# Gate chunks of the modulation move from the weight ring to a ring of three slots on Pool's queue

## What is computed

```python
mod = jax.nn.silu(c) @ w_ada[layer] + b_ada[layer]
shift, scale, gate = jnp.split(mod, 3, axis=-1)
h = rms_norm(x, norm_gain[layer]) * (1.0 + scale[:, None, :]) + shift[:, None, :]
proj = h @ w_in[layer]
q_sb, k_sb, v_sb, z_sb, q_r, k_r, v_r, z_r = jnp.split(proj, split_at, axis=-1)
...            # stick-breaking attention of q_sb, k_sb, v_sb; retention of q_r, k_r, v_r
y = jnp.concatenate([oa, ob], axis=-1).astype(x.dtype) @ w_out[layer]
x = x + (gate[:, None, :] * y).astype(x.dtype)
```

## Time and profile before

| what | value |
|---|---|
| median of three runs | 1970.38 us (1968.21 to 1970.95) |
| profiled execution | 1965.76 us, span 1963.9 us |
| PE busy | 1808.8 us (92%) |
| DVE busy | 1260.0 us (64%) |
| ACT busy | 904.1 us (46%) |
| mean granted clock of PE | 0.961 |
| DMA issue of a weight chunk of `w_in`, 512 KB | lands after 3.8 us (median) |
| DMA issue on POOL's queue into `ada_ring`, 512 KB | lands after 5.9 us (median) |
| DMA issue of `con1`, 836 KB | lands after 5.7 us |

### The profile page before, as it was taken

How to read it: one execution, slowest core, us unless ns; L and a number is a source line. 1 busy time by engine, 2 the same in 40 slices (tenths; PEclk the granted TensorE clock), 3 DMA queues, 4 the chain that set the end, 5 groups by cost and what they waited for, 6 DMA issues and landing times.

```text
span 1963.9 us, 23699 instructions
## 1 busy us (share of the span) xinstructions
PE 1808.8 (92%) x9667; PEld 1531.2 (78%) x9667; DVE 1260.0 (64%) x1604; ACT 904.1 (46%) x1158; POOL 101.3 (5%) x114
## 2 busy tenths in 40 slices
PE   5799987788778998999999999999989999999897
PEld 4688876576556787888888888888878888888786
DVE  5789954564545765578757666785465557667654
ACT  4344432343334543466544456664444555454542
POOL 2311100000000000000000000000000000000000
PEclk8899998899988999999999999999989999999898
DMA  7899955554444454666655455656546565444453
GB/s 263 327 313 342 310 160 186 175 161 150 150 134 123 140 189 144 173 191 191 183 165 148 140 162 160 179 165 193 185 142 187 162 190 151 137 119 119 129 188 112
DMA packets 311835, 350.52 MB, mean 178 GB/s; under 512 B 11232, under 2 KB 286816, under 8 KB 311728
## 3 DMA queue, kind: packets, MB, share of 16 engines
q1 hardware_dynamic: 302400, 315.12, 52.8%
q0 software_dynamic: 9328, 33.89, 4.7%
HBM read 346.87 MB, written 2.10 MB: 178 GB/s over the span
## 4 chain that ended last, share of the span: by engine, by line
PE 77%; DMA 8%; DVE 6%; ACT 5%; issue 3%; SPq 0%; POOL 0%; DVEq 0%; ACTq 0%
PE psG L475 42%; PE psG L476 21%; DMA raw<-in_w_in 7%; ACT w_hi L405 3%; PE psG L469 2%; PE psG L471 2%; PE psG L470 2%; DVE w_lo L409 2%; DVE gate_sum L1145 1%; PE psH L1720 1%; DMA raw<-in_mem_w 1%; PE psH L1734 1%; PE psH L1709 1%; PE psH L2014 1%; PE psH L2015 1%
## 5 line engine op out<-in xcount | busy, mean ns | idle before, releaser
L475 PE MATMUL psG<-xA,w_hi 128*128 128x512 f32 x3392 | 1237.4, 407 | 44.7 <-issue 19.7
L409 DVE TENSOR_TENSOR w_lo<-raw,w_hi 128x1024 fp32r<-128x1024 f32 (+1 forms) x560 | 686.7, 1236 | 438.1 <-ACT w_hi L405 436.3
L476 PE MATMUL psG<-xA,w_lo 128*128 128x256 f32 x3392 | 960.7, 283 | 0.0
L475 PEld LDWEIGHTS psG<-xA,w_hi 128*128 128x128 f32 x3392 | 649.6, 192 | 210.2 <-issue 37.1
L405 ACT ACTIVATE w_hi<-raw 128x1024 fp32r<-128x1024 f32 (+1 forms) x560 | 574.7, 1045 | 493.3 <-DMA raw<-in_w_in 282.5
L476 PEld LDWEIGHTS psG<-xA,w_lo 128*128 128x128 f32 x3392 | 653.4, 193 | 4.2 <-issue 3.6
L444 ACT ACTIVATE P<-psG 128x512 f32<-128x512 f32 x102 | 60.6, 594 | 200.9 <-PE psG L476 200.9
L1098 DVE TENSOR_TENSOR P<-psG,P 128x512 f32<-128x512 f32 (+2 forms) x103 | 70.3, 683 | 106.8 <-ACT P L444 104.6
L1145 DVE SCALAR_TENSOR_TENSOR ada_sum<-ada_ring,silc,ada_sum 128x1024 f32<-128x1024 f32 x60 | 79.5, 1330 | 0.0
L566 POOL TENSOR_TENSOR W<-W 128x512 f32<-128x512 f32 x15 | 22.2, 1483 | 1018.9 <-ACT W L619 1018.9
L475 PE MATMUL psG<-xB,w_hi 128*128 128x512 f32 x192 | 67.6, 396 | 0.0
(11 more groups left out here) (304 smaller groups left out, 1772.1 us busy)
## 6 DMA issues: line engine op xcount, KB each, us to landing
raw<-in_w_in SPq DMA_DIRECT2D x360, 512.0 KB, 3.8
raw<-in_w_out SPq DMA_DIRECT2D x128, 512.0 KB, 3.4
ada_ring<-in_w_ada POOLq DMA_DIRECT2D x64, 512.0 KB, 5.9
raw<-in_mem_w SPq DMA_DIRECT2D x32, 512.0 KB, 8.1
raw<-in_w_ada SPq DMA_DIRECT2D x32, 512.0 KB, 3.9
raw<-in_w_uq SPq DMA_DIRECT2D x24, 384.0 KB, 3.3
raw<-in_w_ukv SPq DMA_DIRECT2D x32, 128.0 KB, 2.4
raw<-in_w_ukv SPq DMA_DIRECT2D x16, 256.0 KB, 3.3
```

The source lines that it names most:

```text
L409: nc.vector.tensor_tensor(low(n), low(n, raw), high(n), ALU.subtract).then_inc(lo_ready, 1)
L475: nc.tensor.matmul(psG[:, bank + f, :], hi[:, w], x, start=first, stop=False)
L476: last = nc.tensor.matmul(psG[:, bank + f, S:2 * S], lo[:, w], x[:, 0:S], start=False, stop=end)
```

## The change

The weight ring holds weights alone. `raw` gets seven slots and `w_hi` five (twelve in all, as before). ACT, before it writes `w_hi` for chunk n, waits until chunk n - 5 is used. The 32 gate chunks are appended to the list that POOL loads; they use three of its six slots, tiles 48, 52 and 56 (`GATE_RING` = 3), and POOL waits for the last user of a slot. DVE's adds stand at other places: every second chunk of `G_SBQK` (8), every chunk of `G_SBV` (8), every second of `G_RTQK` (8), the first eight of `G_RTV` (8). The columns of the first half follow `G_SBV` directly, without the wait for `sb_y` 2; those of the second half follow `G_RTV`, behind the wait for `sb_y` 4 that stood there. As the retention values are written where gate chunks lie, ACT waits for all 96 adds before it takes a product of `G_RTV` (`before_taken`). At the start, `first()` comes before the inverse root on ACT and before the norm on DVE.

```diff
-SLOTS = 6
+SLOTS, HIGH_SLOTS = 7, 5
+GATE_RING = 3
-        w_hi = sb("w_hi", [NP, SLOTS, 1024], F32R)
+        w_hi = sb("w_hi", [NP, HIGH_SLOTS, 1024], F32R)
-        GATE_AT = {G_SBQK: lambda i: i % 2 == 1, G_SBV: lambda i: i % 2 == 1, G_RTQK: lambda i: i % 4 == 3,
-                   G_RTV: lambda i: i % 2 == 1, G_SBZ: lambda i: i % 2 == 1}
+        GATE_AT = {G_SBQK: lambda i: i % 2 == 1, G_SBV: lambda i: True, G_RTQK: lambda i: i % 2 == 1, G_RTV: lambda i: i < 8}
+        ITEMS = [("weight", n) for n in range(len(CHUNKS))]
+        ADA_SLOT = [m % len(ADA_RING) for m in range(2 * ADA_HALF)] + [m % GATE_RING for m in range(ADA_HALF)]
...
                 if j >= SLOTS:
-                    before, m = ITEMS[j - SLOTS]
-                    sp.wait_ge(*((chunk_used, m + 1) if before == "weight" else (ada_used, 2 * ADA_HALF + m + 1)))
-                if kind == "gate":
-                    k, half = m_to_gate(n)
-                    sp.dma_start(raw[:, j % SLOTS, :], ada_rows(k, 2, half)).then_inc(raw_loaded[j % SLOTS], 16)
-                    continue
+                    sp.wait_ge(chunk_used, ITEMS[j - SLOTS][1] + 1)
...
         def split_hi(act, n):
             arrived(act, "weight", n)
+            if n >= HIGH_SLOTS:
+                act.wait_ge(chunk_used, n + 1 - HIGH_SLOTS)
...
-                if m >= len(ADA_RING):
-                    pool.wait_ge(ada_used, m + 1 - len(ADA_RING))
+                if ADA_BEFORE[m] is not None:
+                    pool.wait_ge(ada_used, ADA_BEFORE[m] + 1)
                 pool.dma_start(ada_ring[slot][:, :], ada_rows(k, part, half)).then_inc(ada_loaded[slot], 16)
...
+            first()
             norm_inverse_root(0)
-            first()
...
-            run(G_RTV, lambda b, p: sb_hook(2 + b, p))
+            run(G_RTV, lambda b, p: sb_hook(2 + b, p), before_taken=lambda: act.wait_ge(ada_used, 3 * ADA_HALF))
...
-            norm(0, mem_raw, V("mem_norm", 0, 16), between=between)
+            first()
+            norm(0, mem_raw, V("mem_norm", 0, 16))
...
             run_products(pe, G_SBV)
+            gate_columns(0)
             pe.wait_ge(loaded["con1"], 16)
...
             run_products(pe, G_RTQK, sb_hook)
-            pe.wait_ge(q["sb_y"], 2)
-            gate_columns(0)
             run_products(pe, G_RTV, lambda b, p: sb_hook(2 + b, p))
             pe.wait_ge(q["sb_y"], 4)
+            gate_columns(1)
...
             run_products(pe, G_SBZ, rt_hook)
-            pe.wait_ge(q["rt_y"], 2)
-            gate_columns(1)
```

More of the change, by code:

```diff
@@ L338, in build @@
         BLOCKS = [(g, b) for g in ORDER for b in range(g.blocks)]
-        GATE_AT = {G_SBQK: lambda i: i % 2 == 1, G_SBV: lambda i: i % 2 == 1, G_RTQK: lambda i: i % 4 == 3,
-                   G_RTV: lambda i: i % 2 == 1, G_SBZ: lambda i: i % 2 == 1}
[L343 to L348, removed]
+        GATE_AT = {G_SBQK: lambda i: i % 2 == 1, G_SBV: lambda i: True, G_RTQK: lambda i: i % 2 == 1, G_RTV: lambda i: i < 8}
+        GATE_UNITS = [g.c0 + i for g in ORDER if g in GATE_AT for i in range(len(g.order)) if GATE_AT[g](i)]
+        ITEMS = [("weight", n) for n in range(len(CHUNKS))]
         PLACE, LOADS = {}, []
         for j, (kind, n) in enumerate(ITEMS):
-            by_tile = kind == "weight" and CHUNKS[n][0].by_tile
+            by_tile = CHUNKS[n][0].by_tile
             LOADS.append((LOADS[j - SLOTS] if j >= SLOTS else 0) + (CHUNKS[n][0].kk if by_tile else 1))
             PLACE[kind, n] = j
+        ADA_SLOT = [m % len(ADA_RING) for m in range(2 * ADA_HALF)] + [m % GATE_RING for m in range(ADA_HALF)]
+        ADA_BEFORE = [max([i for i in range(m) if ADA_SLOT[i] == ADA_SLOT[m]], default=None) for m in range(3 * ADA_HALF)]
+        ADA_COUNT = [ADA_SLOT[:m + 1].count(ADA_SLOT[m]) for m in range(3 * ADA_HALF)]
         def arrived(eng, kind, n):
@@ L369, in high @@
             g = CHUNKS[n][0]
-            return w_hi[:, n % SLOTS, 0:g.kk * g.cols]
+            return w_hi[:, n % HIGH_SLOTS, 0:g.kk * g.cols]
         def low(n, t=None):
@@ L398, in ada_rows @@
             return io["w_ada"][NP * k:NP * k + NP, c0:c0 + D_MODEL // 2]
-        def m_to_gate(m):
-            return m % KT, m // KT
         def split_hi(act, n):
             arrived(act, "weight", n)
+            if n >= HIGH_SLOTS:
+                act.wait_ge(chunk_used, n + 1 - HIGH_SLOTS)
             nc.scalar.activation(high(n), low(n, raw), ACT.Copy).then_inc(hi_ready, 1)
@@ L489, in build @@
         sb_v, rt_v = (tiles(t, 8).rearrange("p (h f) -> p h f", h=2) for t in (SBV, RTV))
-        ADA_ORDER = [(half, k, part) for half in range(2) for k in range(KT) for part in range(2)]
+        ADA_ORDER = [(half, k, part) for half in range(2) for k in range(KT) for part in range(2)] + [
+            (half, k, 2) for half in range(2) for k in range(KT)]
         GATED1 = [(SBQ, SBZ), (SBQ + 4, SBZ + 4), (RTQ, RTZ), (RTQ + 4, RTZ + 4)]
@@ L571, in _ @@
             for m, (half, k, part) in enumerate(ADA_ORDER):
-                slot = m % len(ADA_RING)
+                slot = ADA_SLOT[m]
                 if m == 20:
                     add_squares(1)
-                if m >= len(ADA_RING):
-                    pool.wait_ge(ada_used, m + 1 - len(ADA_RING))
+                if ADA_BEFORE[m] is not None:
+                    pool.wait_ge(ada_used, ADA_BEFORE[m] + 1)
                 pool.dma_start(ada_ring[slot][:, :], ada_rows(k, part, half)).then_inc(ada_loaded[slot], 16)
@@ L670, in first, with run, block_done @@
                     split_hi(act, n)
-            def run(g, hook=no_hook, hook_first=True):
-                run_split(act, split_hi, g, hook, hook_first, lambda b: take_product(act, g, b))
+            def run(g, hook=no_hook, hook_first=True, before_taken=lambda: None):
+                def block_done(b):
+                    before_taken()
+                    take_product(act, g, b)
+                run_split(act, split_hi, g, hook, hook_first, block_done)
             act.wait_ge(loaded["vec"], 16)
@@ L1070, in norm_step, with norm @@
                                                in1=x[:, 0:S], op0=ALU.add, op1=ALU.subtract).then_inc(q["nm_lo"], 1)
-            def norm(n, src, gain, between=None):
+            def norm(n, src, gain):
                 dve.wait_ge(q["nm_rs"], n + 1)
                 for t in range(KT + 2):
-                    if between:
-                        between(t)
                     norm_step(n, src, gain, None, t, 0, KT)
@@ L1125, in ada_add @@
             def ada_add(m):
[L1127 to L1140, removed]
+                half, k, part = ADA_ORDER[m]
+                dve.wait_ge(ada_loaded[ADA_SLOT[m]], 16 * ADA_COUNT[m])
+                src, out = ada_ring[ADA_SLOT[m]][:, :], ada_sum[:, part, :] if part < 2 else gate_sum[:, :]
+                if k == 0 and half:
+                    dve.wait_ge(q["ada_cols" if part < 2 else "gate_cols"], 1)
                 if k == 0:
@@ L1146, in ada_add @@
                                            op1=ALU.add).then_inc(ada_used, 1)
-            def between(t):
-                if t == 4:
-                    first()
-            norm(0, mem_raw, V("mem_norm", 0, 16), between=between)
+            first()
+            norm(0, mem_raw, V("mem_norm", 0, 16))
             def modulation(half):
@@ L1199, in hook @@
                     if p % 2 and GATE_AT[g](i):
-                        ada_add(2 * ADA_HALF + ITEMS[PLACE["weight", g.c0 + i] + 1][1])
+                        ada_add(2 * ADA_HALF + GATE_UNITS.index(g.c0 + i))
                 return hook
@@ L1304, in z1_hook @@
                     gate_1(n - 1)
-            run(G_SBZ, both(z1_hook, gate_hook(G_SBZ)))
-            gate_columns(1)
+            run(G_SBZ, z1_hook)
             run(G_RTZ, lambda b, p: z1_hook(2 + b, p))
```

## The result

| | before | after |
|---|---|---|
| median | 1969.3 us | 1844.2 us |
| profiled execution, span | 1963.9 us | 1842.6 us |
| PE busy | 1808.8 us (92%) | 1768.5 us (96%) |
| mean granted clock of PE | 0.961 | 0.984 |

The ratio is 0.9367, with a 95% interval from 0.9351 to 0.9384: 6.3% or 125 us less, where 97 were forecast. The median before has one run more in it than the one that the forecast started from (1970.4).

The account below looks back on a forecast made before the run. The prediction took a loop of DMA, ACT and DVE through gate chunks in the weight ring as the bound. Gains of 32 + 37 + 23 + 5 = 97 us gave 1869, as median 1873 us; 8 in 10: 1852 to 1908.

Parts of the forecast that it names:

- What bound the kernel before: From 258 to 618 us: a loop of DMA, ACT and DVE through late-released gate chunks, 4.6 us per chunk against PE's 2.81.
- `G_SBQK` and `G_SBV`: First matmul of G_SBQK to first hook step: 79 us instead of 111.1, 32 us gained, between 15 and 38.
- The 342 GB/s: Load rate used to price bandwidth: 9.2 MB in G_SBV take 27 us, 5 too many; 2 us booked.
- `G_RTQK`, `G_RTV`: Hook groups with sb_hook: 31 us per group, sum 125 us instead of 148.2, 23 us gained, between 10 and 30.
- The wait of ACT for the 96th add: End of the first group of G_RTV: ACT waits for DVE before taking the product, costing 1 us, at most 3.
- `G_SBZ`: Two groups with rt_hook at 30 us each: 60 us instead of 97.5, 37 us gained.
- The start: Splits moved ahead of the norm's root: PE starts at about 26.2 us, not 31.10; 5 us gained, from 0 to 6.5.
- The seventh slot: Outside the gate stretches loads aren't late on PE's path, so it is worth 0 to 2 us there.
- The three slots: Rival: POOL's three gate slots turn too slowly in G_SBV and G_RTV, 15 to 45 us lost, about 1900; chance 0.24.
- The rule: GpSimd can't write load descriptors during VectorE's two-port ops, so POOL's gate loads could come a DVE op later; chance 0.08.
- The hooks as the bound all along: Rival: the hooks' loop between PE, ACT and DVE was the bound; only the start gains, 1955 to 1968; chance 0.04.
- The five high slots, as a loss on every chunk: Rival: ACT held back everywhere, all 560 chunks pay 0.25 us each, 140 us lost, 2013; chance 0.05.

Follow-up runs that it names:

- e5: Kernel before, with DVE adding a gate chunk ahead of the split, not behind it; same ring, loads and work: 1916.0 us, ratio 0.9734.
- e3: Changed kernel with six raw and six high slots and the old start, so the gate chunks' move alone: 1859.6 us, ratio 0.9441.
- e1: Kernel before with only the early start: first() ahead of the inverse root on ACT and of the norm on DVE: 1963.7 us, ratio 0.9974.
- e8: Changed kernel, early start kept, with six raw and six high slots: 1859.6 us, ratio 0.9447.
- e4: Changed kernel without the early start: 1849.0 us, ratio 0.9389.
- e12: Changed kernel run once more, unaltered, as a measure of scatter: 1847.5 us, ratio 0.9371.
- e6: Changed kernel with two slots for gate chunks, not three: 1854.6 us, ratio 0.9416.
- e7: Changed kernel with eight raw and four high slots: 1851.0 us, ratio 0.9395.
- e2: Kernel before with seven raw and five high slots, gate chunks still in the ring, old start: 1894.6 us, ratio 0.9625.
- e10: Kernel before with gate loads of 128 columns in place of 1024 (64 KB, not 512), gate not computed: 1946.1 us, ratio 0.9886.

## Where the prediction was right, and which of its steps failed

**What bound the kernel before: right.** The late release in a shared ring is shown by e5, which moves only DVE's add and takes `G_SBQK` and `G_SBV` from 111 to 83 us, and by e3, which takes the gate chunks out (with their adds and columns), leaves slots and start as they were, and brings 110 us. What the prediction didn't see is what looks like a second loop in the hook groups, through PE. It changes nothing in the forecast for the change, as the groups are as short in e3 as after.

**The sum, term by term,** on the profiled executions (121.3 us measured, 97 forecast):

- `G_SBQK` and `G_SBV`: 32 forecast, 35.6 measured (124.5 - 88.9). From the first matmul of `G_SBQK` it took 73.9 us, not 79, a gain of 37.2; the stage has 1.6 less, as the stretch ahead of `G_SBQK` is longer by that, at the clock of 0.77. I had booked 2 us for bandwidth and 5 for the gate columns. The columns took 1.95 and PE's wait 0.7. The 342 GB/s that I had taken as the rate of loads is no limit either (see the last section). DVE at 85% was no burden.
- `G_RTQK`, `G_RTV`: 23 forecast, 31.3 measured. **This size failed.** A group takes 29.5, 29.5 and 29.3 us, not the 31 that I took, and the last with the columns 28.5. The 31 was my 29.3 with a surcharge for DVE's hook steps behind adds. Its only row was the whole stretch 618 to 680, and no row priced the hook steps; PE's waits for them are 2.3 us in all, and 0.8 more ahead of the second columns. That 29.3 came so close was also luck: it is a group of `rt_hook` with some clock loss in it, and at the full clock such a group takes 28.4. The wait of ACT for the 96th add, 1 us in the sum, took ACT 4.4 us and PE none: the group behind it is no longer than the others.
- `G_SBZ`: 37 forecast, 40.5 measured; groups of 28.5, not 30. `G_RTZ` gained 0.9 that I hadn't counted, as the group that I took for my measure (29.3 us) had itself some clock loss: 0.97, and 1.00 after.
- The start: 5 forecast. The first matmul comes 6.0 us earlier, and e1 gives the edit 5 us of the whole. Measured up to the first columns are 9.7 (6.0 and 3.7), with the seventh slot in it. DVE's timeline after shows the mechanism as forecast, the splits ahead of the root and the tiles right behind it:

```profile
15.57 3.50 DVE L402 TENSOR_TENSOR w_lo<-raw,w_hi 128x1024 fp32r<-128x1024 f32 x3 [11.39 <-ACT w_hi L398]
21.24 1.27 DVE L1059 SCALAR_TENSOR_TENSOR W<-P,vec,W 128x256 f32<-128x256 f32 x3 [2.17 <-ACT W L634]
```

- The seventh slot: **this step failed.** "Outside these stretches loads aren't late on PE's path, so a seventh slot is worth 0 to 2 us there", with 1.5 in the sum, at the start. It is worth 10 to 15 us (e8 against after, e3 against e4), in the two stretches where loads set the pace. Up to the first hook step it is 11.0 us (339.7 in e8, 328.7 after), and with six slots these stretches gain 34.4 us, a little under the 37 forecast. The start stretch of the kernel before has 12 us of PE's idle time and a clock of 0.90, and I had read it only for its end:

```profile
31.00:101.00 70.00, 57.88 (x267) 48.03 (x268) 57.35 (x63) 27.59 (x35) 21.27 (x26) 0.90 0.83 299
```

- The rest: 3.2 us, of which e12 shows 2.8 to be scatter between executions.

So the excess of 24 us is 3.6 + 8.3 + 4.4 + 4.7 + 3.2: half of it (8.3 + 4.4) are the groups that I took too long, a third (3.6 + 4.7) the stretches in which the seventh slot counts. The forecast median was off by 29 us. The other 4.6 are the distance between the profiled execution and the median, which I had added because it was there before; after the change the median (1844.2) lies 0.2 us under the profiled execution (1844.4).

**The range.** Its low end came from "PE's idle and clock loss removed in full", 118 us. That ceiling was taken over 258 to 618 us and held only 5 us for everything else. Inside, 107 of its 113 us came (35.6 + 31.3 + 40.5); outside, 14 us came and not 5. The start stretch, which the change touches twice, has its own idle time, and the ceiling had to hold it. The surcharges without rows then moved the likeliest value to the wrong side of the middle.

**The rivals.** The three slots: not at three (0.8 us of waits for landing), but at two (e6). The rule that the prediction cites from the Trainium skill, "SBUF — State Buffer", section "SBUF: two separate sides", would have made POOL's loads later while DVE works in such a mode. The gate loads of the kernel after (253 to 445 us) land as follows:

```profile
DMA to landing us min/median/max: 4.0/5.0/7.2
```

Before, the same queue's loads landed after 4.7/5.7/6.7 us from 132 to 258 us, so no added delay is seen, with DVE busy for 75 to 85% of the time. The 4.0/7.5/9.9 of the earlier trace rows belong to the start, and there the kernel after still has 4.5/8.5/11.0 (25 to 80 us). As the profile doesn't say whether DVE's operations here ran in a two-port mode, this shows that these operations did no harm, and not that the rule is wrong. The hooks as the bound all along: refuted by e3, since the groups fall to 29.5 and 28.5 with only the gate chunks moved. The five high slots, as a loss on every chunk: refuted even for four (e7).

## What to carry to other kernels

In a ring that is issued in order, what matters is when the slowest user releases its slot, counted in items, more than how many bytes pass or how busy the engines are: one position of an add was worth 51 us, gate loads of an eighth of the size 24, and taking the slow users out of the ring 110, at the same number of slots. Read the lap from the chain (landing, split, add, issue) and divide it by the items it covers; if that exceeds the compute engine's time per item, the ring is the bound. And when a change deepens a ring, price it in every stretch where loads are late, not only in the one that the change is about; surcharges for contention that no row shows are better put into the range than into the sum.

## What the runs showed of the hardware that was not expected

A weight load of 512 KB lands after 3.8 us when the gate load of the same size is issued 1.0 us behind it (e2), and after 5.3 us, or 6.0 in the next lap, when it is issued 0.4 us ahead of it (before); with a gate load of 64 KB ahead it is 4.0 (e10).

Loads reached 393 GB/s over 25 us of the kernel after (first row below), and 391 over 35 us in e7 with eight slots, where e8 with six had 317. So the 342 GB/s by which the prediction priced loads was no limit.

And DMA at 364 GB/s and DVE at 89% cost PE nothing, which is never idle beside them: from 90 to 122 us of the kernel after (second row).

```profile
35.00:60.00 25.00, 21.08 (x105) 17.37 (x104) 23.88 (x23) 9.36 (x11) 6.34 (x12) 0.93 1.04 393
90.00:122.00 32.00, 32.00 (x167) 27.37 (x166) 28.41 (x26) 14.18 (x16) 5.82 (x11) 1.00 1.02 364
```
